# The fused transformer blocks on one core: value chunks cut as half the features by 512 outputs, in adjacent pairs

## What is computed

```python
proj = h @ w_in                                   # 1024 -> cq, ckv, k_rope, fq, fk, fv (512), ...
o_fox = causal_block_attention(fq, fk, fv, FOX_SCALE, f_cum)
...
q, k, v = jnp.split(h @ w_in, 3, axis=-1)         # each of layers 0 and 1: v is 1024 wide
o = softmax(scores(q, k)) @ v
h = h + o @ w_out
```

## Time and profile before

| | |
|---|---|
| median of three executions | 1031.52 us |
| the profiled execution | 1030.44 us |
| its span | 1028.7 us |
| PE matmul / PE weight load busy | 1013.8 us / 987.4 us |
| DVE / ACT busy | 686.1 us / 575.3 us |
| mean granted TensorE clock | 0.996 of full |

### The profile page before, as it was taken

The page is one execution under the profiler, slowest core; times in us unless marked ns, Lnnn a source line. Parts: engine busy times, 40 slices in busy tenths (PEclk is TensorE's granted clock), DMA queues, the critical chain, the costliest instruction groups (busy, mean ns, idle before and its releaser), DMA issues.

```text
span 1028.7 us, 19890 instructions
## 1 busy us (share of the span) xinstructions
PE 1013.8 (99%) x8368; PEld 987.4 (96%) x8368; DVE 686.1 (67%) x1155; ACT 575.3 (56%) x954; POOL 0.4 (0%) x5
## 2 busy tenths in 40 slices
PE   8999999999999999999999999999999999999997
PEld 7899899999999999999999999999999999999997
DVE  4797888868888676887567555455766377545542
ACT  4778565647555556767647444444665465544442
POOL 0000000000000000000000000000000000000000
PEclk9999999999999999999999999999999999999999
DMA  9865567435666544543236554545633336545411
GB/s 384 346 249 212 214 237 307 185 123 206 228 259 246 194 154 185 205 174 131 111 124 235 177 197 170 193 176 187 248 140 131 117 119 259 196 168 201 167 40 41
DMA packets 27880, 196.42 MB, mean 191 GB/s; under 512 B 3088, under 2 KB 3728, under 8 KB 4496
## 3 DMA queue, kind: packets, MB, share of 16 engines
q1 hardware_dynamic: 27216, 194.43, 50.7%
q10 hardware_dynamic: 576, 0.72, 0.2%
HBM read 194.09 MB, written 1.05 MB: 190 GB/s over the span
## 4 chain that ended last, share of the span: by engine, by line
PE 87%; DVE 7%; ACT 3%; DMA 2%; issue 1%; SPq 0%; DVEq 0%; ACTq 0%
PE PS L959 22%; PE PS L960 22%; PE PS L961 22%; PE PS L1124 3%; PE PS L1127 3%; PE PS L1125 3%; DVE wlo L1724 3%; DMA raw<-wall 2%; PE PS L1172 2%; PE PS L1173 1%; PE PS L1174 1%; PE PS L1298 1%; PE PS L1320 1%; PE PS L1287 1%; PE PS L1286 1%
## 5 line engine op out<-in xcount | busy, mean ns | idle before, releaser
L1724 DVE TENSOR_TENSOR wlo<-raw,whi 128x1024 fp32r<-128x1024 f32 (+1 forms) x314 | 368.1, 1216 | 124.4 <-ACT whi L1363 124.3
L1363 ACT ACTIVATE whi<-raw 128x1024 fp32r<-128x1024 f32 x308 | 307.3, 1048 | 169.4 <-PE PS L961 164.2
L959 PE MATMUL PS<-Hh,whi 128*128 128x256 f32 x1232 | 353.6, 287 | 4.5 <-ACT GA L1559 2.2
L960 PE MATMUL PS<-Hl,whi 128*128 128x256 f32 x1232 | 349.2, 283 | 0.0
L961 PE MATMUL PS<-Hh,wlo 128*128 128x256 f32 x1232 | 349.1, 283 | 0.0
L959 PEld LDWEIGHTS PS<-Hh,whi 128*128 128x128 f32 x1232 | 236.9, 192 | 11.1 <-issue 7.4
L960 PEld LDWEIGHTS PS<-Hl,whi 128*128 128x128 f32 x1232 | 237.0, 192 | 0.2
L961 PEld LDWEIGHTS PS<-Hh,wlo 128*128 128x128 f32 x1232 | 236.9, 192 | 0.0
L959 PE MATMUL PS<-Oh,whi 128*128 128x256 f32 x816 | 231.1, 283 | 0.0
L961 PE MATMUL PS<-Oh,wlo 128*128 128x256 f32 x816 | 231.0, 283 | 0.0
L960 PE MATMUL PS<-Ol,whi 128*128 128x256 f32 x816 | 231.0, 283 | 0.0
(11 more groups left out here) (246 smaller groups left out, 1161.4 us busy)
## 6 DMA issues: line engine op xcount, KB each, us to landing
raw<-wall SPq DMA_DIRECT2D x155, 1024.0 KB, 4.8
raw<-wada SPq DMA_DIRECT2D x18, 1024.0 KB, 5.1
GA<-wada SPq DMA_DIRECT2D x2, 1024.0 KB, 19.3
GA<-alibi SPq DMA_DIRECT2D x1, 2048.0 KB, 9.2
raw<-wall SPq DMA_DIRECT2D x2, 768.0 KB, 5.9
X<-xt SPq DMA_DIRECT2D x1, 1024.0 KB, 5.2
KM<-wada SPq DMA_DIRECT2D x1, 1024.0 KB, 14.8
QF<-wada SPq DMA_DIRECT2D x1, 1024.0 KB, 16.8
```

The source lines that it names most:

```text
L959: e.matmul(dst, wh, a, start=start, stop=False, skip_group_check=share)
L960: e.matmul(dst, wh, b, start=False, stop=False, skip_group_check=share)
L1363: e.activation(whi[place(n)][:, c], raw[i % RAW][:, c], ACT.Copy).then_inc(*up("a_whi", (n, half)))
L1724: e.tensor_tensor(wlo[place(n)][:, c], raw[i % RAW][:, c], f32(whi[place(n)][:, c]), ALU.subtract).then_inc(*up("v_wlo", (n, half)))
```

## The change

Six of the ten value chunks (`in 7`, `in 8`, and `qkv 8` and `qkv 9` of both layers) are packed as 512 features by 512 outputs in place of 1024 by 256. A new step `token_half` multiplies one such chunk, for each of two token tiles in its own bank, with 12 matmuls of 512 columns; the second chunk of a pair adds to the same two banks, which are given out before the first and emptied after the second. `ev_vf` and the new `ev_v_halves` empty both banks, with two copies of 512 columns. `QKV_ORDER` puts chunk 9 right behind chunk 8. Chunks 10 and 11 stay as they were. Between `in 7` and `in 8` the chunk `uq 1` stays where it was.

```diff
@@ -49,7 +49,10 @@
 
 NCOL = _columns()
 
-QKV_ORDER = (0, 4, 1, 5, 8, 2, 6, 9, 3, 7, 10, 11)
+QKV_ORDER = (0, 4, 1, 5, 8, 9, 2, 6, 3, 7, 10, 11)
+
+
+BY_HALVES = [("in", 7), ("in", 8)] + [(f"qkv{layer}", c) for layer in range(2) for c in (8, 9)]
 
 
 def weight_order():
@@ -231,6 +234,20 @@
         emit("tokens", n, src, b, 1)
         st["done"] = n
         evac(n, b)
+        after()
+        if fill:
+            refill(n)
+
+    def token_half(key, src, bs, half, evac=None, fill=True):
+
+        n = NUMBER[key]
+        ensure(n)
+        emit("token_half", n, src, bs[0], half, 0)
+        middle()
+        emit("token_half", n, src, bs[1], half, 1)
+        st["done"] = n
+        if evac:
+            evac(n)
         after()
         if fill:
             refill(n)
@@ -369,10 +386,11 @@
 
     rows(("uq", 0), "lat", pairs=2, mid=False, evac=lambda n, b, pr: emit("ev_queries", n, b, pr))
     heads["all"].append(("fox", 0))
-    tokens(("in", 7), "mix", lambda n, b: emit("ev_vf", n, b, 0))
+    fv = [bank(), bank()]
+    token_half(("in", 7), "mix", fv, 0)
     rows(("uq", 1), "lat", pairs=2, mid=False, evac=ev_uq_rope)
     heads["all"].append(("fox", 1))
-    tokens(("in", 8), "mix", lambda n, b: emit("ev_vf", n, b, 1), fill=False)
+    token_half(("in", 8), "mix", fv, 1, lambda n: emit("ev_vf", n, *fv), fill=False)
     n = NUMBER[("ukv", 0)]
     ensure(n)
     for pr in range(2):
@@ -548,6 +566,15 @@
             elif c < 8:
                 rows(key, a, evac=lambda n, b, pr, c=c: emit("ev_qk", n, b, layer, "K", c - 4))
                 heads["all"] += [(kind, 2 * (c - 4)), (kind, 2 * (c - 4) + 1)]
+            elif c < 10:
+                if c == 8:
+                    vs = [bank(), bank()]
+
+                def ev_halves(n):
+                    emit("ev_v_halves", n, *vs, layer)
+                    have_v.extend((0, 1))
+
+                token_half(key, a, vs, c - 8, ev_halves if c == 9 else None)
             else:
                 def ev_v(n, b, c=c):
                     emit("ev_v", n, b, layer, c - 8)
@@ -1175,6 +1202,22 @@
                 if half == 1:
                     m.then_inc(*up("t_mm", (n, 0)))
                     marks.at["t_mm", n] = marks.at["t_mm", (n, 0)]
+            elif step == "token_half":
+                n, src, b, half, t = a
+                slot = place(n)
+                if half == 0:
+                    bank(b)
+                for k in range(4):
+                    weights_there(n, k * 512 + 512)
+                    split_there(split_key(src, 4 * half + k))
+                    c = slice(k * 512, k * 512 + 512)
+                    hi, lo = (x[:, 4 * half + k, t * 128:t * 128 + 128] for x in (Hh, Hl))
+                    e.matmul(PS[:, b, :], hi, whi[slot][:, c], start=half == 0 and k == 0, stop=False, skip_group_check=True)
+                    e.matmul(PS[:, b, :], lo, whi[slot][:, c], start=False, stop=False, skip_group_check=True)
+                    m = e.matmul(
+                        PS[:, b, :], hi, wlo[slot][:, c], start=False, stop=half == 1 and k == 3, skip_group_check=True)
+                m.then_inc(*up("t_mm", (n, t)))
+                marks.at["t_mm", n] = marks.at["t_mm", (n, t)]
             elif step == "ukv_values":
                 n, b, half = a
                 slot = place(n)
@@ -1226,8 +1269,10 @@
 
             elif step in ("ev_cq", "ev_cq_ff_kr", "ev_ckv"):
                 free[a[1]] = ("a_ev", (FIRST, a[1]))
-            elif step in ("ev_gate", "ev_vf", "ev_v"):
+            elif step in ("ev_gate", "ev_v"):
                 free[a[1]] = ("a_ev", (a[0], 0))
+            elif step in ("ev_vf", "ev_v_halves"):
+                free[a[1]], free[a[2]] = ("a_ev", (a[0], 0)), ("a_ev", (a[0], 1))
             elif step == "ev_heads":
                 free[a[1]] = ("a_ev", (a[0], a[2]))
             elif step == "ev_queries":
@@ -1303,16 +1348,16 @@
                 kind, i = head
                 for j, slot in enumerate(slots(head)[:1 if kind == "diff" else 2]):
                     if kind == "diff":
-                        on.wait_ge("a_ev", (NUMBER[("qkv0", 8 + i // 2)], 0))
+                        on.wait_ge("a_ev", (NUMBER[("qkv0", 8 + i // 2)], 0) if i > 3 else (NUMBER[("qkv0", 9)], 1))
                         v, dst = V[:, :, i * 128:i * 128 + 128], PS[:, OB, 0:256]
                     else:
                         h = 2 * i + j
                         if kind == "fox":
-                            on.wait_ge("a_ev", (NUMBER[("in", 7 + h // 4)], 0))
+                            on.wait_ge("a_ev", (NUMBER[("in", 8)], 1))
                         elif kind == "mla":
                             on.wait_ge("a_ev", (NUMBER[("ukv", 0)], 3))
                         else:
-                            on.wait_ge("a_ev", (NUMBER[("qkv1", 8 + h // 4)], 0))
+                            on.wait_ge("a_ev", (NUMBER[("qkv1", 8 + h // 4)], 0) if h > 7 else (NUMBER[("qkv1", 9)], 1))
                         v = {"fox": VF, "mla": VM, "moba": V}[kind][:, :, h * 64:(h + 1) * 64]
                         dst = PS[64 * j:64 * j + 64, OB, 0:256]
                     on.wait_ge("a_t", (head, slot))
@@ -1543,11 +1588,10 @@
                 m.then_inc(*up("a_qr", 0))
                 sq_free[0] = sq_free[1] = ("v_qr", "sum")
             elif step == "ev_vf":
-                n, b, j = a
-                on.wait_ge("t_mm", (n, 0))
-                e.activation(
-                    VF[:, :, 256 * j:256 * j + 256], PS[:, b, :].rearrange("p (h n) -> p h n", h=2), ACT.Copy).then_inc(
-                    *up("a_ev", (n, 0)))
+                n, b0, b1 = a
+                for t, b in enumerate((b0, b1)):
+                    on.wait_ge("t_mm", (n, t))
+                    e.activation(VF[:, t, :], PS[:, b, :], ACT.Copy).then_inc(*up("a_ev", (n, t)))
             elif step == "ev_vm":
                 n, b, half = a
                 on.wait_ge("t_mm", (n, 2 + half))
@@ -1620,6 +1664,12 @@
                 e.activation(LM[:, 2:4], LM[:, 0:2], ACT.Exp).then_inc(*up("a_lam", 0))
             elif step == "ev_qk":
                 rb_free[0] = ("v_qk", tuple(a[2:]))
+            elif step == "ev_v_halves":
+                n, b0, b1, layer = a
+                on.wait_ge("v_rec" if layer else "v_r", "a1" if layer else "both")
+                for t, b in enumerate((b0, b1)):
+                    on.wait_ge("t_mm", (n, t))
+                    e.activation(V[:, t, 0:512], PS[:, b, :], ACT.Copy, scale=ST[:, t:t + 1]).then_inc(*up("a_ev", (n, t)))
             elif step == "ev_v":
                 n, b, layer, j = a
                 on.wait_ge("t_mm", (n, 0))
@@ -2192,6 +2242,8 @@
         c = r(256 * i, 256 * i + 256)
         if kind == "first":
             t = _tiles(a["w_in"][0][c], cols_in[0:1024])
+        elif (kind, i) in BY_HALVES and kind == "in":
+            t = _tiles(a["w_in"][0][512 * (i - 7):512 * (i - 7) + 512], cols_in[1792:2304])
         elif kind == "in":
             t = _tiles(a["w_in"][0], cols_in[c])
         elif kind == "uq":
@@ -2209,7 +2261,10 @@
         else:
             layer = int(kind[-1])
             w = a[{"qkv": "w_in_2", "out": "w_out_2", "ff1": "w_ff1_2", "ff2": "w_ff2_2"}[kind[:-1]]][layer]
-            t = _tiles(w[c], r(1024)) if kind[:-1] == "ff2" else _tiles(w, c)
+            if (kind, i) in BY_HALVES:
+                t = _tiles(w[512 * (i - 8):512 * (i - 8) + 512], 2048 + r(512))
+            else:
+                t = _tiles(w[c], r(1024)) if kind[:-1] == "ff2" else _tiles(w, c)
         out.append(t)
     return np.stack(out)
```

## The result

Slower: a median of 1034.51 us (1033.72 to 1036.85, 6 executions) against 1031.76 (1030.49 to 1032.07, 6 executions). The ratio is 1.0031, with a 95% interval of 1.0021 to 1.0041: 2.75 us more on the medians, 2.2 to 4.2 by the interval. The profiled execution took 1036.03 us, span 1034.2.

A forecast was written before the change was run, and what follows sets the result against it. PE, busy 99% of the span, was taken as the bound, with an ACT, DVE, ACT chain through the fox stage. 1.94 + 0 + 0.7 - 0.72 = +1.9 us on the median gave 1033.4 us, range 1031.0 to 1035.5.

The forecast's parts named there:

- the case to which I gave 0.44: Whole kernel: a result slower than before by more than 0.2%, chance 0.44.
- my own: Whole kernel: +1.9 us, 1033.4 us, no change that can be told, on the slow side; chance 0.5.
- the rival with one more fall: Pauses at ukv and in 10: both, or the new one twice over, bring low clock; 1034.9 us, slower; chance 0.24.
- that rival's sign: Before in 10: the second pause again as long as the old 2.21 us, and the clock low behind both pauses.
- the sum said 1.9: Whole kernel: wait 1.94, clock 0, layer 0 0.7, wider matmuls -0.72, together +1.9 us.
- A wait in front of ukv, +1.94: Before ukv, PE waits for ACT to empty the fox banks; ACT's later copy starts 1.94 us late; bounds 0 and 3.1.
- The clock, net 0: One 1.5 us fall to 1.2 GHz moves from before in 10 to ukv; net 0, bounds -1.5 and +1.5.
- My rival with a fall "twice over": At ukv: the new pause brings the low clock twice over; 1034.9 us, in a rival of chance 0.24.
- Layer 0, +0.7: Layer 0: sub_out and head 4's scaling stand behind emptying q chunk 3; PE waits 0.7 us more, bounds 0 and 1.0.
- Fewer, wider matmuls, -0.36 a pair: Value chunks: 512-column matmuls take 232.5 ns against 240; 0.36 us saved a pair, 0.72 in layers 0 and 1.
- The 131 ns of the Trainium skill: Layers' value chunks: the page's figure per 512-column matmul in a stream would save 10.5 us; the trace showed 232.5 ns.
- the rival of the 120 ns: Layers' value chunks: wide matmuls take 120 ns in a long stream; 11.5 us less, near 1022 us; chance 0.01.

The follow-up runs named there:

- change_filled: The changed kernel with 32 idle matmuls on PE in the pause in front of ukv; 1033.42 us, ratio 1.0015 to the kernel before.
- before_filled: The kernel before with 16 idle matmuls on PE in the pause before in 10; 1030.63 us, ratio 0.9990.
- fox_alone: The changed kernel with only the fox pair by halves, both layers as in the kernel before; 1035.34 us, ratio 1.0036 to the kernel before.
- order_alone: The kernel before with only the new order of chunks, all value chunks 1024 by 256; 1032.14 us, ratio 1.0009.
- layer1_all_four: The kernel before with new order and halves in layer 1 only, chunks 10 and 11 also a pair by halves; 1029.91 us, ratio 0.9983.
- best_of_parts: The changed kernel with ukv rows in banks 1 and 2, count restored behind in 10, 16 idle matmuls before it, layer 0 as before; 1030.24 us.
- banks_restored: The changed kernel with the ukv row pairs in banks 1 and 2 and the bank count set back behind in 10; 1032.32 us, ratio 1.0003.

## Why the prediction was right and wrong

The time lay inside the range, and the result in the case to which I gave 0.44, not in my own: it is slower by more than 0.2%, 1.1 us above the 1033.4 I named. That is near the 1034.9 of the rival with one more fall, but that rival's sign did not come: the second pause was 1.16 us and no low clock followed it. In the traces the change costs 3.0 us where the sum said 1.9, and more of the surplus lies in layer 0 (1.50 against 0.7 - 0.36) than in the clock (+0.7 against 0); layer 1 gave 0.3 more back than I counted, and the late start of this execution gave another 0.3. By its steps:

**A wait in front of ukv, +1.94: right**, 1.83 by change_filled against before_filled. ACT's timeline with the change, to be set against the earlier trace rows:

```profile
98.50 1.06 ACT L1594 ACTIVATE V<-PS 128x512 f32<-128x512 f32 x2
101.13 0.59 ACT L1558 ACTIVATE KM<-PS 64x512 f32<-64x512 f32 x1 [1.58 <-PE PS L988]
...
105.17 0.60 ACT L1599 ACTIVATE V<-PS 128x512 f32<-128x512 f32 x1 [0.28 <-PE PS L1232]
...
116.59 0.57 ACT L1603 ACTIVATE GA<-PS 128x512 f32<-128x512 f32 x1
```

ACT's first copy comes at 98.50, not 97.84, so this execution, which had begun the stage 1.09 late, was 0.66 late there; fox_alone, which was on time, had PE go on at 98.19. Each later row lags more, by the low clock. I had PE go on at 115.08; with 0.66 and the 1.5 of a fall that is 117.24, and it went on at 117.22. PE stood idle 3.98 us in front of `ukv` and 1.16 before `in 10`, where I had said a pause of some 4.2 and 1.0.

**The clock, net 0: one of the two steps that failed.** I took one fall of 1.5 us to move from the old pause to the new. It did move, but what it gave back is not what it cost. The old fall gave back 0.8, because 0.7 went into the wait at `in 13`, where the prediction had no term at all. The new one costs 2.19 - 0.72 = 1.5 in the change's profile, and 3.16 - 0.71 = 2.45 in fox_alone, where the low stretch is twice as long (of which some 0.3 is that kernel's start on time). So the step is worth +0.7 with the short stretch and about +1.4 with the long one. My rival with a fall "twice over" names the long stretch; it came in two of the three profiles with an unfilled pause. Why the change had the short one was not settled.

**Layer 0, +0.7: the other step that failed, too small by more than half.** The wait at head 4 came as worked out (0.87 us of idle time, about 1 was forecast). I followed this head and stopped. The waits at heads 5 and 6, 1.2 us together, come with the new order, as order_alone shows (1.9 us of waits at heads 4 and 5 by the order alone, where before had 0.4 in all); that it is the three turnings in a row is my reading of the list. By the distances between starts the waits at the turnings take 1.8 us more than before and the steps right behind them some 0.2; with the 0.5 saved that makes the 1.5 measured.

**Fewer, wider matmuls, -0.36 a pair: right in kind, too small.** 0.52 us (the second pair of layer1_all_four). The four steps of the earlier trace rows had been too few: 228.9 ns, not 232.5. The 131 ns of the Trainium skill ("TensorE: Matmul & The Clock Gate", "Back-to-back issue gap") is nowhere near in these long streams either, and the rival of the 120 ns is out. By 239.4 - 228.9 for each of 48 it is 0.50 us. The fox pair I had counted at nothing, and best_of_parts bears that out.

The terms as the traces give them: the wait +1.83, the old fall -0.80, the new one +1.47, the late start -0.31, layer 0 +1.50, layer 1 -0.66: +3.0, beside 2.75 on the medians. The four of the fox stage add up to its 2.19 by the way they are taken; what stands by itself is that the slow steps behind the fall cost 1.5 us before (3.53 against 2.02), and that the late start is worth 0.31 to 0.39 in two other kernels.

## What to carry to other kernels

A bank (or any buffer) that is held longer is paid for by its next user: look who that is, and what stands in front of the engine that empties it; and when the rotation of the banks is shifted by a count, read every later place that takes from the same rotation. A pause on TensorE can have two prices, the chain's and the clock's, and in three kernels here idle matmuls in it took away the second. Where two chains run nearly level, time won on one is in part a wait at their next meeting, so a term is followed to the next place where the engines meet, and a reordering to the last item that it delays.

## What the runs showed of the hardware

- The clock fell to 1.2 GHz without a pause: at 55.9 to 57.2 us in 8 of the 14 profiles, at a place that none of the edits touches. Before it PE had made 16 and 4 products with a single column, rows of 1.84 and 0.58 us in the change. The same 20 products stand in front of that place in all 14 profiles, and in six the clock stayed full, so they don't decide it alone:

```profile
53.55 1.84 PE L995 MATMUL PS<-ONES,SQ 128*128 128x1 f32 x16
55.26 0.58 PE L995 MATMUL PS<-ONES,V 128*128 128x1 f32 x4
```

- The same pause of 2.2 us before `in 10` (2.47 to 2.49 us between two starts) was followed by a low clock in 5 of 7 profiles and by none in order_alone and banks_restored. Of one kernel's executions those with the lower mean granted clock are the longer (order_alone: 1030.57 us at 0.999, 1032.14 at 0.996, 1035.05 at 0.991), and a fall costs about 1.5 us, so effects under a microsecond are read in the traces' starts rather than in medians.
- An idle stretch in front of work can lie in the low clock as well: in fox_alone it was low from 96.26, 1.9 us before PE went on.
